# Split parts of x over four banks with a wait for each, and another order of work at both ends of each feed-forward network

## The reference

```python
def swiglu(x, w_gate, w_up, w_down):
    return (jax.nn.silu(x @ w_gate) * (x @ w_up)) @ w_down
...
    h = rmsnorm(x, ffn1_norm[l])
    x = x + 0.5 * swiglu_2(h, ffn1_w_gate[l], ffn1_w_up[l], ffn1_w_down[l])
    h = rmsnorm(x, mix_norm[l])
    ...
    h = rmsnorm(x, cross_norm[l])
    ...
    h = rmsnorm(x, ffn2_norm[l])
    x = x + 0.5 * swiglu_2(h, ffn2_w_gate[l], ffn2_w_up[l], ffn2_w_down[l])
```

## Time and profile before

| what | value |
|---|---|
| three executions | 2123.05, 2126.62, 2126.33 us, median 2126.33 |
| the profiled execution | 2124.94 us, of which the span is 2123.2 |
| PE busy | 2021.8 us (95% of the span) |
| DVE, ACT, POOL busy | 1510.3, 1238.6, 98.0 us |
| chain that ended last, by engine | PE 90%, DVE 6%, ACT 3%, issue 1% |
| DMA | 258 GB/s in the mean |

### The profile page before, as it was taken

One profiled execution on the slowest core, in us unless ns is written; L12 is line 12 of the kernel. 1 busy time (PEld: TensorE's weight loads), 2 busy tenths in 40 slices (PEclk: granted clock), 3 DMA queues, 4 the chain that ended last, 5 costly groups with the idle time before them and its releaser, 6 DMA issues.

```text
span 2123.2 us, 26423 instructions
## 1 busy us (share of the span) xinstructions
PE 2021.8 (95%) x9638; PEld 1684.8 (79%) x9638; DVE 1510.3 (71%) x1515; ACT 1238.6 (58%) x1288; POOL 98.0 (5%) x99
## 2 busy tenths in 40 slices
PE   6989998997999999999999999998999999989997
PEld 6877887876888888888888888876788798777886
DVE  5675455667899899989889998997555555545453
ACT  5444444544777777777777777765544444434433
POOL 1000000001000000000000000130200030000000
PEclk9999999997999999999999999999999999999999
DMA  7337554335999999999999999997555443434550
GB/s 315 112 128 279 184 184 143 129 120 183 370 382 383 375 383 380 385 369 384 372 385 375 384 381 366 392 378 284 190 197 179 148 158 125 156 127 160 197 178 20
DMA packets 78662, 548.72 MB, mean 258 GB/s; under 512 B 8992, under 2 KB 8992, under 8 KB 16896
## 3 DMA queue, kind: packets, MB, share of 16 engines
q1 hardware_dynamic: 72864, 519.77, 65.4%
q0 software_dynamic: 5712, 27.77, 3.5%
HBM read 540.68 MB, written 10.49 MB: 260 GB/s over the span
## 4 chain that ended last, share of the span: by engine, by line
PE 90%; DVE 6%; ACT 3%; issue 1%; DMA 0%; POOL 0%; DVEq 0%; ACTq 0%; POOLq 0%
PE ps L532 28%; PE ps L534 27%; PE ps L533 27%; DVE wlo L1682 2%; PE ps L735 1%; ACT whi L1272 1%; PE ps L667 1%; DVE resid L1741 0%; PE ps L1013 0%; PE ps L1034 0%; DVE r L1737 0%; ACT xth L1290 0%; PE ps L1041 0%; PE ps L548 0%; PE ps L1058 0%
## 5 line engine op out<-in xcount | busy, mean ns | idle before, releaser
L1682 DVE TENSOR_TENSOR wlo<-raw,whi 128x2048 fp32r<-128x2048 f32 (+4 forms) x506 | 1148.6, 2273 | 342.7 <-ACT whi L1272 338.1
L1272 ACT ACTIVATE whi<-raw 128x2048 fp32r<-128x2048 f32 (+4 forms) x506 | 950.2, 1880 | 209.3 <-PE ps L534 206.5
L532 PE MATMUL ps<-whi,xth 128*128 128x512 f32 (+3 forms) x1888 | 750.6, 398 | 23.0 <-DVE wlo L1682 6.5
L534 PE MATMUL ps<-whi,xtl 128*128 128x512 f32 (+3 forms) x1888 | 731.1, 387 | 0.0
L533 PE MATMUL ps<-wlo,xth 128*128 128x512 f32 (+3 forms) x1888 | 729.7, 386 | 0.0
L532 PEld LDWEIGHTS ps<-whi,xth 128*128 128x128 f32 x1888 | 359.7, 190 | 94.6 <-issue 16.5
L534 PEld LDWEIGHTS ps<-whi,xtl 128*128 128x128 f32 x1888 | 359.4, 190 | 70.2
L533 PEld LDWEIGHTS ps<-wlo,xth 128*128 128x128 f32 x1888 | 360.4, 191 | 62.8
L532 PE MATMUL ps<-whi,hth 128*128 128x512 f32 (+2 forms) x736 | 287.5, 391 | 6.6 <-DVE htl L1799 4.5
L534 PE MATMUL ps<-whi,htl 128*128 128x512 f32 (+2 forms) x736 | 286.1, 389 | 0.0
L533 PE MATMUL ps<-wlo,hth 128*128 128x512 f32 (+2 forms) x736 | 285.0, 387 | 0.0
(11 more groups left out here) (321 smaller groups left out, 1238.6 us busy)
## 6 DMA issues: line engine op xcount, KB each, us to landing
raw<-in_stream SPq DMA_DIRECT2D x475, 1024.0 KB, 7.0
raw<-in_stream SPq DMA_DIRECT2D x16, 768.0 KB, 4.4
bc<-in_rows POOLq DMA_DIRECT2D x5, 1024.0 KB, 5.1
slot_rows<-in_blank POOLq DMA_DIRECT2D x7, 512.0 KB, 8.8
kc<-slot_rows POOLq DMA_DIRECT2D x7, 512.0 KB, 9.0
sum_rows<-r POOLq DMA_DIRECT2D x7, 512.0 KB, 8.5
raw<-in_stream SPq DMA_DIRECT2D x4, 832.0 KB, 5.0
raw<-in_stream SPq DMA_DIRECT2D x4, 640.0 KB, 3.9
```

What stands on the lines that cost most here:

```text
L532: pe.matmul(o, ah, bh, start=start, stop=False, skip_group_check=True)
L534: return pe.matmul(o, al, bh, start=False, stop=stop, skip_group_check=True)
L1272: act.activation(whi[:, c.split, 0:c.width], raw[:, c.raw, 0:c.width], ACT.Copy).then_inc(hi_done, 1)
L1682: dve.tensor_tensor(wlo[:, c.split, 0:c.width], raw[:, c.raw, 0:c.width], f32(whi[:, c.split, 0:c.width]), ALU.subtract).then_inc(lo_done, 1)
```

## The change

It has three parts; the engines' arithmetic is the same.

1. Stages `n1`, `nmix`, `mix2`, `ncross`, `n2` (`SPREAD`) use `transpose_spread`: parts k and k + 4 share one of four banks, `tr` rises after each such pair of tile 1, and ACT's split, DVE's split and PE's start wait for each part alone. From part 4 on ACT also waits until DVE has read the part that shares the bank. `n1` and `n2` turn in banks 2 to 5 instead of 0 to 3.
2. `second_unit`: in each FFN PE starts unit 1 (in banks 3 and 1) right behind unit 0, and `turn(0)` comes after the first 12 of its matmuls.
3. `last_unit`: in the last unit `down` of the unit before goes by tile, with the turn of the same tile of the last unit behind it (bank 2 for tile 0, 3 for tile 1); ACT and DVE split each tile alone, and the last `down` waits per tile.

```diff
@@ -92,6 +92,9 @@
...
+SPREAD = ("n1", "nmix", "mix2", "ncross", "n2")
...
@@ -195,7 +198,7 @@
     (n, 1) for n in ("n1", "nmem", "nmix", "mix2", "ncross", "n2")]
 UNIT_KINDS = ("sg", "hu", "ut", "hh", "ht")
 for _k, _c in (("sg", T), ("hu", T), ("ut", 1), ("hh", 1), ("ht", 1)):
-    RAISED[_k] = [(n, _c * u) for n, u in _ffns]
+    RAISED[_k] = [(n, _c * u + (_c == 1)) for n, u in _ffns]
...
@@ -538,7 +541,21 @@
 
             def split_done(stage, k):
 
-                pe.wait_ge(*at(stage, "xt", (k // 2 + 1) * dict(RAISED["xt"])[stage] // (KD // 2)))
+                if stage in SPREAD:
+                    pe.wait_ge(*at(stage, "xt", k + 1))
+                else:
+                    pe.wait_ge(*at(stage, "xt", (k // 2 + 1) * dict(RAISED["xt"])[stage] // (KD // 2)))
+
+            def transpose_spread(stage, src, banks, ready):
+
+                for t in range(T):
+                    pe.wait_ge(*ready(t))
+                    for b in range(4):
+                        for k in (b, b + 4):
+                            m = pe.transpose(ps[banks[b]][:, (k // 4) * S + t * P:(k // 4) * S + (t + 1) * P],
+                                             src[:, t, k * P:(k + 1) * P], ident)
+                        if t == T - 1:
+                            m.then_inc(sem("tr"), 1)
...
@@ -645,12 +662,16 @@
                                         wh[:, k, :], wl[:, k, :], start=(kk == 0), stop=(kk == 7))
                         m.then_inc(used, 1)
 
-                def down(c, u, first, last):
-                    chunk(c)
-                    pe.wait_ge(*at(name, "ht", u + 1))
+                def down(c, u, first, last, tiles=range(T)):
+                    if 0 in tiles:
+                        chunk(c)
+                    if not last:
+                        pe.wait_ge(*at(name, "ht", u + 1))
                     wh = whi[:, c.split, :].rearrange("p (k n) -> p k n", k=2)
                     wl = wlo[:, c.split, :].rearrange("p (k n) -> p k n", k=2)
-                    for t in range(T):
+                    for t in tiles:
+                        if last:
+                            pe.wait_ge(*at(name, "ht", u + 1 + t))
                         for n in range(2):
                             for k in range(2):
                                 m = mm3(ps[4 + 2 * t + n][:, :], hth[:, k, t * P:(t + 1) * P], htl[:, k, t * P:(t + 1) * P],
@@ -658,7 +679,8 @@
                                         start=first and k == 0, stop=last and k == 1)
                         if last and t == 0 and name != "f1":
                             m.then_inc(sem(f"first_tile_{name}"), 1)
-                    m.then_inc(used, 1)
+                    if T - 1 in tiles:
+                        m.then_inc(used, 1)
...
+                def second_unit(a, b, c):
+
+                    for j, w in enumerate((a, b)):
+                        chunk(w)
+                        wh = whi[:, w.split, :].rearrange("p (k n) -> p k n", k=4)
+                        wl = wlo[:, w.split, :].rearrange("p (k n) -> p k n", k=4)
+                        for t in range(T):
+                            for k in range(4):
+                                kk = 4 * j + k
+                                m = mm3(ps[(3, 1)[t]][:, :], xth[:, kk, t * P:(t + 1) * P], xtl[:, kk, t * P:(t + 1) * P],
+                                        wh[:, k, :], wl[:, k, :], start=(kk == 0), stop=(kk == 7))
+                            if (j, t) == (0, 0):
+                                turn(0)
+                        m.then_inc(used, 1)
+                    down(c, 0, True, False)
+                    turn(1)
+
+                def turn_part(u, t):
+
+                    pe.wait_ge(*at(name, "hu", 2 * u + 1 + t))
+                    for k in range(2):
+                        m = pe.transpose(ps[2 + t][:, k * P:(k + 1) * P], hs[:, t, k * P:(k + 1) * P], ident)
+                    m.then_inc(unit_sem(name, "ut"), 1)
+
+                def last_unit(u, base):
+
+                    gate_up(Chunk(base), Chunk(base + 1))
+                    for t in range(T):
+                        down(Chunk(base + 2), u - 1, False, False, (t,))
+                        turn_part(u, t)
+
...
-                turn(0)
-                unit(1, first_chunk + 2, 0, True)
+                second_unit(*(Chunk(first_chunk + 2 + n) for n in range(3)))
                 loops = (units - 3) // UNROLL
                 with pe.Fori(0, loops) as it:
                     for j in range(UNROLL):
                         unit(it * UNROLL + 2 + j, first_chunk + 5 + 3 * j, it, False)
-                for u in range(2 + loops * UNROLL, units):
+                for u in range(2 + loops * UNROLL, units - 1):
                     unit(u, first_chunk + 3 * u - 1, 0, False)
+                last_unit(units - 1, first_chunk + 3 * units - 4)
...
-            transpose_x("n1", x, ready=lambda t: at("ln2_1", "x", t + 1))
+            transpose_spread("n1", x, TURN_BANKS, lambda t: at("ln2_1", "x", t + 1))
             ffn("f2", U_FF, "n1")
-            transpose_x("nmix", x, ready=lambda t: at("f2", "resid", 2 * t + 2))
+            transpose_spread("nmix", x, (0, 1, 2, 3), lambda t: at("f2", "resid", 2 * t + 2))
...
-                transpose_x("mix2", r, KD, TURN_BANKS)
+                transpose_spread("mix2", r, TURN_BANKS, lambda t: at("mix2", "x", t + 1))
...
-            transpose_x("ncross", x, KD, TURN_BANKS, ready=lambda t: at("out2", "resid", 2 * t + 2))
+            transpose_spread("ncross", x, TURN_BANKS, lambda t: at("out2", "resid", 2 * t + 2))
...
-            transpose_x("n2", x, ready=lambda t: at("xo", "resid", 2 * t + 2))
+            transpose_spread("n2", x, TURN_BANKS, lambda t: at("xo", "resid", 2 * t + 2))
...
             def split_x(stage, gain=None, kn=KD, dst=xth, banks=(0, 1, 2, 3)):
 
+                if stage in SPREAD:
+                    for k in range(KD):
+                        act.wait_ge(*at(stage, "tr", k % 4 + 1))
+                        if k >= 4:
+                            act.wait_ge(*at(stage, "xt", k - 3))
+                        act.activation(xth[:, k, :], ps[banks[k % 4]][:, (k // 4) * S:(k // 4 + 1) * S], ACT.Copy,
+                                       scale=cols[:, gain + k:gain + k + 1]).then_inc(sem("xh"), 1)
+                    return
...
-                def unit(u, base, it, chunks):
+                def unit(u, base, it, chunks, banks=(0, 1), last=False):
...
-                        act.activation(sg[:, t, :], ps[t][:, 0:FU], ACT.Silu,
+                        act.activation(sg[:, t, :], ps[banks[t]][:, 0:FU], ACT.Silu,
                                        scale=rstd[:, t:t + 1] if scaled else 1.0).then_inc(unit_sem(name, "sg"), 1)
                     if n + chunks - 1 < NCHUNK:
                         hi(Chunk(n + chunks - 1, it))
+                    if last:
+                        for t in range(T):
+                            act.wait_ge(*at(name, "ut", u + 1 + t))
+                            act.activation(hth[:, 0:2, t * P:(t + 1) * P], ps[2 + t][:, 0:S].rearrange("p (k s) -> p k s", k=2),
+                                           ACT.Copy).then_inc(unit_sem(name, "hh"), 1)
+                        return
...
-                unit(1, first_chunk + 2, 0, 3)
+                unit(1, first_chunk + 2, 0, 3, banks=(3, 1))
...
-                    unit(u, first_chunk + 3 * u - 1, 0, 3)
+                    unit(u, first_chunk + 3 * u - 1, 0, 3, last=u == units - 1)
...
-            split_x("n1", COLS["ffn1"])
+            split_x("n1", COLS["ffn1"], banks=TURN_BANKS)
...
+                if stage in SPREAD:
+                    for k in range(KD):
+                        dve.wait_ge(*at(stage, "xh", k + 1))
+                        dve.scalar_tensor_tensor(out=xtl[:, k, :], in0=ps[banks[k % 4]][:, (k // 4) * S:(k // 4 + 1) * S],
+                                                 scalar=cols[:, gain + k:gain + k + 1], in1=f32(xth[:, k, :]),
+                                                 op0=ALU.mult, op1=ALU.subtract).then_inc(sem("xt"), 1)
+                    return
...
                             m = dve.scalar_tensor_tensor(out=hs[:, t, :], in0=sg[:, t, :], scalar=rstd[:, t:t + 1],
-                                                         in1=ps[t][:, FU:2 * FU], op0=ALU.mult, op1=ALU.mult)
...
+                    if last:
+                        for t in range(T):
+                            dve.wait_ge(*at(name, "hh", u + 1 + t))
+                            dve.tensor_tensor(htl[:, 0:2, t * P:(t + 1) * P], ps[2 + t][:, 0:S].rearrange("p (k s) -> p k s", k=2),
+                                              f32(hth[:, 0:2, t * P:(t + 1) * P]), ALU.subtract).then_inc(unit_sem(name, "ht"), 1)
+                        return
```

More of the change, by code:

```diff
@@ L1662, in _ @@
             advance(AT["xo"] + 3 + LEAD)
-            split_x("n2", COLS["ffn2"])
+            split_x("n2", COLS["ffn2"], banks=TURN_BANKS)
```

(6 more changed lines are left out.)

7 lines of the change are left out of this document (4 added, 3 removed).

## The result

| | median | lowest to highest | ratio to before, 95% interval |
|---|---|---|---|
| before (six runs) | 2126.47 us | 2123.05 to 2128.19 | |
| the change (six runs) | 2114.77 us | 2111.66 to 2119.49 | 0.9947 (0.9936 to 0.9958) |
| the change once more, later (five runs; before 2124.97) | 2115.78 us | 2115.28 to 2119.64 | 0.9958 (0.9944 to 0.9971) |

11.7 us faster in the first comparison, 9.2 in the second. Forecast were 2115.1 us in a range of 2110.5 to 2120.5, and 0.9 for faster by over 0.2%. The profiled execution took 2115.82 us (span 2114.0).

A forecast was written before the change was run, and what follows sets the result against it. PE carries 90% of the chain, so only its idle waits, 17.9 us, could be gained. Terms 4.7 + 4.1 + 2.4 = 11.2 us off 2126.33 gave 2115.1 us, range 2110.5 to 2120.5.

The forecast's parts named there:

- the pot: PE's waits at the edited places, for `xtl`, `htl` and DVE's product: 17.9 us in all that could be gained.
- Second unit: Unit 0 to unit 1 of each FFN: 12 matmuls cover PE's stall, 1.42 + 1.64 + 1.63 = 4.7 us gained.
- chunk 3: Unit 1 of `f2`: its `lo` ends at 1507.84, PE wants it at 1508.5, 0.7 us of room left.
- Last unit by tile: End of each FFN: waits for `htl` shrink, `f0` 0.7, `f2` 1.7, `f3` 1.7, sum 4.1 us.
- The tight place in `f2`: Last unit: DVE's half for tile 0, behind a chunk's `lo`, fits by 0.3 us, or 0.15 with the signal's way.
- DVE's halves: Low part by tile: 418 ns each against 692 whole, 0.14 us more per FFN, beside PE and charged nothing.
- Spread split: x in four banks: `n2` and `mix2` 0.76 each, `ncross` 0.7, `n1` 0.2, `nmix` 0; sum 2.4 us.
- Rival 4: Clock falls to 1.2 GHz at nine of eleven edited places, costing 19.8 us: 8.6 us slower, 2134.9; chance 0.03.
- the loop: FFN loops: a chunk's supply sets the pace and takes the gain back, some 3 us stay, 2123 us; chance 0.05.
- ACT's eight parts: ACT's split of x: starts and ends as before, 3.03 us; more than 3.1 would be a sign of being wrong.
- rival 1: Parts bring their own waits: split gains nothing, chunk 3 and `f2`'s half late; 7.5 us gained, 2118.8; chance 0.15.
- Rival 2: Everything behind the late piece moves too: `f0` gives 1.7, the split 3.8; 13.6 us gained, 2112.7; chance 0.07.

The follow-up runs named there:

- second_alone: Kernel before with only the second unit begun ahead of the first's turn: 2122.49 us, ratio 0.9979.
- lo_later: Changed kernel with DVE's low part of layer 1's chunk, ahead of the first sum behind `f0`, moved behind tile 0's split: 2114.47 us, ratio 0.9951.
- experiment 3: Changed kernel once more, unedited: 2115.78 us, ratio 0.9958. Lost clock was summed over 2 us windows reading below 0.95, as 2 us times one minus the clock.
- nmix_only: Kernel before with the spread split in `nmix` alone: 2125.01 us, one run.
- no_nmix: Changed kernel with `nmix` taken out of the spread split: 2115.97 us, ratio 0.9956; a second profile took 2113.45 us, one run.
- experiment 1: Kernel before with each part of the change by itself: second unit 2122.49 us, last unit by tile 2120.94, spread split 2125.39.
- hi_first: Changed kernel with ACT's `hi` of the second chunk ahead of the split of x in `n1` and `nmix`: ratios 0.9921, then 0.9930; median 2109.54 us.
- spread_alone: Kernel before with only the spread split, including the two banks of `n1` and `n2`: 2125.39 us, ratio 0.9998.
- last_alone: Kernel before with only the last unit by tile: 2120.94 us, ratio 0.9981.

## Why the prediction was right

The time came out 0.3 us from the forecast. That close is luck: the changed kernel's own eleven runs spread over 8 us. What can be judged are the terms.

- **What bounds it.** PE's waits were the pot, and for the two parts at the ends of the FFNs what they lost is what the kernel gained. Right.
- **Second unit, 4.7 us.** 5.0 in the stretches of `second_alone`, 4.5 in its runs. The cover (12 matmuls over a stall of 1.4 to 1.6) and the next thing late (chunk 3, 0.7 us of room; 0.6 seen) are both in the timeline.
- **Last unit by tile, 4.1 us.** 4.27 and 4.0. The step that needed care was `f0`: 0.7 forecast, 0.75 measured, and `lo_later` got the other 0.97. The tight place in `f2` had 0.33 us, of a forecast 0.15 to 0.3. In both parts `f2` came out 0.15 to 0.18 us above its stall; in `n1` 6.8 us of clock were lost (summed as in experiment 3) in the profile of before and 5.1 in these two. `nmix_only`, where `f2` is unedited, has 5.1 too and is 0.12 us shorter there, so this is the clock's and not the parts'.
- **DVE's halves.** They take 418 to 425 ns, as the earlier trace rows had it. `f3` gave 4.12 us against 0.76 + 1.63 + 1.70 = 4.09, so the 0.14 us that two halves cost is hidden. The Trainium skill (Advanced Engine Details and Errata, TRN2 Errata) advises tiles of 512 or 1024 elements on ScalarE and VectorE. The rows agree that a half costs more than half; on PE's path that would have been 0.4 us, and beside PE it cost nothing.
- **Spread split, 2.4 us.** `n2` 0.74, `ncross` 0.75, `mix2` 0.75 off its wait, `nmix` 0, and `n1` 0.08 where 0.2 was taken: 2.3. The 0.08 is the clock's in the profile of before; against the three other profiles with the old split `n1` lost 0.19, because the prediction had ACT end when it did, and with the clock at 0.50 it does not. That leaves 2.1. The wait for `wlo` in `n1` came out 0.63 where 0.3 was named. And the waits for `xtl` were not all 1.36: at `mix2` it was 1.93 and is 1.17, the same step off a longer wait. The part alone measured 0.4 us, with 2.3 at the edge of its interval. This term is right as waits removed in four of its five places and unproven as time gained.
- **Rival 4, the clock** (0.03). Its mechanism came at one place of the eleven, `nmix`, and cost 1.4 us. Six would have been needed for a slower kernel, and eight for one slower by the prediction's own 0.2% ((11.2 + 4.3) / 2.2). The argument against it, that the clock had stayed at 1.00 through a stall of 1.70 us, was too weak: in `no_nmix` it fell behind 1.35 us, and in `nmix_only` it held through 2.41. The length of one wait does not say whether it falls.
- **Rivals 1 to 3.** No new wait on chunk 3, the loop as before (PE 40.00 of 40 us in the window 1560 to 1600). ACT's eight parts took 3.03 us in `nmix`, as before, but 3.21 in `n1`, where they had taken 3.03: that is over the 3.1 named as a sign of rival 1. It cost 0.19 us there (experiment 1), and rival 1 had the split gain nothing at all. Rival 2's larger `f0` term did not come without a further edit.

The six stretches of the changed kernel are 2.22 + 3.32 - 0.01 + 0.02 + 0.74 + 4.12 = 10.4 us shorter than before. Against 11.2 forecast the missing 0.8 lies between `nmix` and `mix2`. There `mix2` gave 0.75 and the fall in `nmix` took 1.4. The profile of before has a fall at 1770 us that the changed kernel's lacks, which gives back some of it; how much is not shown.

**What stays open.** Why the clock falls in `nmix`. It fell there in all six profiles that have the spread split in `n1` and not `hi_first`'s moves (the change twice, `spread_alone`, `lo_later`, `no_nmix` twice), and in none of the four that have the old split in `n1` (before, `second_alone`, `last_alone`, `nmix_only`), nor in the four with `hi_first`'s moves. That it hangs on what comes before `f2`, 190 us earlier, is only what this count suggests; `n1` alone in the spread form was not run.
